# Expert layers: the two transfers of an expert's down weights issued by ScalarE on its own queue instead of by SyncE

## What is computed

```
# hier_moe: 32 experts of hidden size 512, top 2 per token; 512 tokens in layer 0, 256 in layer 1
expert_id, weights = route(h)                  # softmax over 4 groups, top 2 of the 8 experts of the best group
for each expert e with its tokens xb:          # w_gate[e], w_up[e]: 1024x512, w_down[e]: 512x1024
    y = (silu(xb @ w_gate[e]) * (xb @ w_up[e])) @ w_down[e]
out = sum over a token's two experts of weight * y
```

## Time and profile before

| | us |
|---|---|
| median of 3 runs | 3430.38 |
| lowest, highest | 3428.68, 3433.78 |
| span of the profiled execution | 3434.0 |
| PE busy in it | 2861.8 (83%) |
| PE weight loads busy | 1999.7 (58%) |
| DVE, ACT, POOL busy | 1089.5, 506.6, 253.4 |
| moved by DMA | 643.13 MB, of it 539.04 on SP's queue and 75.93 on ACT's |

### The profile page before, as it was taken

One profiled execution on the slowest core, in us unless ns is written; L12 is line 12 of the kernel. 1 busy time (PEld: TensorE's weight loads), 2 busy tenths in 40 slices (PEclk: granted clock), 3 DMA queues, 4 the chain that ended last, 5 costly groups with the idle time before them and its releaser, 6 DMA issues. The chain is left out here.

```text
span 3434.0 us, 58306 instructions
## 1 busy us (share of the span) xinstructions
PE 2861.8 (83%) x25537; PEld 1999.7 (58%) x25537; DVE 1089.5 (32%) x2184; ACT 506.6 (15%) x1104; POOL 253.4 (7%) x277
## 2 busy tenths in 40 slices
PE   6999989899898896877777379798889977877774
PEld 5887745788784444444444134388888864444442
DVE  3562363255514413100000231356556422000002
ACT  1000122100010101000000100154444310000000
POOL 0000000000000000100000110032322201000000
PEclk9999765898999997999999689799999978999997
DMA  6784120476523206899999411000000039999994
GB/s 214 236 253 133 50 92 1 136 257 185 181 74 110 62 25 239 320 390 394 396 395 400 155 62 46 18 4 4 4 3 4 4 133 380 390 398 391 395 393 167
DMA packets 284675, 643.13 MB, mean 187 GB/s; under 512 B 23540, under 2 KB 176676, under 8 KB 250772
## 3 DMA queue, kind: packets, MB, share of 16 engines
q1 hardware_dynamic: 237152, 539.04, 43.1%
q10 hardware_dynamic: 39556, 75.93, 6.1%
q0 software_dynamic: 7728, 24.59, 2.3%
HBM read 612.73 MB, written 26.77 MB: 186 GB/s over the span
## 5 line engine op out<-in xcount | busy, mean ns | idle before, releaser
L1888 PE MATMUL bank<-expert_weights,ex_xt 128*64 128x256 f32 x2688 | 352.1, 422 | 103.6 <-DMA expert_weights<-in_moe_w_up_dram 103.4
L1888 PEld LDWEIGHTS bank<-expert_weights,ex_xt 128*64 128x64 f32 x2688 | 237.6, 153 | 232.7 <-issue 160.9
L448 PE MATMUL bank<-u,weights 128*128 128x272 f32 (+1 forms) x1408 | 318.7, 390 | 14.0 <-DVEq L471 14.0
L448 PEld LDWEIGHTS bank<-u,weights 128*128 128x128 f32 x1408 | 270.8, 192 | 61.9 <-DVEq L471 14.8
L1840 DVE TENSOR_TENSOR ex_hidden<-ex_silu,bank 128x256 f32<-128x256 f32 x64 | 27.0, 422 | 685.0 <-ACT ex_silu L1924 685.0
L1888 PE MATMUL bank<-weights,ex_xt 128*64 128x256 f32 x1408 | 184.9, 423 | 58.5 <-DMA weights<-in_moe_w_up_dram 57.1
L1168 DVE SCALAR_TENSOR_TENSOR ada_acc<-ada_w,cond,ada_acc 128x512 f32 (+1 forms) x336 | 227.6, 746 | 1.5 <-PEq L420 1.5
L526 PE MATMUL bank<-rw_mixed,weights 128*128 128x512 f32 (+2 forms) x448 | 189.0, 583 | 31.7 <-DVEq L537 28.2
L1888 PEld LDWEIGHTS bank<-weights,ex_xt 128*64 128x64 f32 x1408 | 123.6, 153 | 126.5 <-issue 89.4
L1909 PE MATMUL bank<-expert_weights,ex_hidden_turned 128*64 128x512 f32 x672 | 153.5, 598 | 21.7 <-DVE ex_hidden_turned L1843 21.7
L1924 ACT ACTIVATE ex_silu<-bank 128x256 f32<-128x256 f32 x64 | 24.5, 383 | 957.7 <-PE bank L1888 957.7
(11 more groups left out here) (507 smaller groups left out, 4108.5 us busy)
## 6 DMA issues: line engine op xcount, KB each, us to landing
expert_weights<-in_moe_w_gate_dram SPq DMA_DIRECT2D x84, 1024.0 KB, 25.9
expert_weights<-in_moe_w_up_dram SPq DMA_DIRECT2D x84, 1024.0 KB, 26.6
expert_weights<-in_moe_w_down_dram SPq DMA_DIRECT2D x84, 1024.0 KB, 25.8
ada_w<-in_ada_w_dram ACTq DMA_DIRECT2D x24, 2048.0 KB, 8.8
weights<-in_moe_w_gate_dram SPq DMA_DIRECT2D x44, 1024.0 KB, 25.7
weights<-in_moe_w_up_dram SPq DMA_DIRECT2D x44, 1024.0 KB, 26.3
weights<-in_moe_w_down_dram SPq DMA_DIRECT2D x44, 1024.0 KB, 25.9
weights<-in_w_gate_dram SPq DMA_DIRECT2D x22, 1024.0 KB, 5.5
```

The source lines that it names most:

```text
L448: last = nc.tensor.matmul(k.bank[b + side * NB][:, 0:N], w[:, f, c * P:(c + 1) * P], rhs[:, f, 0:N], start=(f == 5), stop=(f == 4))
L1888: last = nc.tensor.matmul(half_cols(k.bank[2 + side], t), xt[:, s, f * SLOTS:(f + 1) * SLOTS], w[:, q * 512 + t * 256:q * 512 + t * 256 + ...
```

## The change

The loop over pieces on SP ends at piece 3 in `experts_stage`. ACT's function gets, between the copy of the tokens of e + 1 and the wait for `kept`, the issue of pieces 4 and 5 of expert e + 2, for e from 1 to 29, behind a wait for `spent` at 4(e - 1) + 4. ACT's block also moves ahead of PE's in the source, because `ring.start` enters in a table, while the program is built, the semaphore value that PE's `ring.wait` reads.

```diff
@@ block.sync
             for e in range(3, NE):
-                for j in range(ring.PIECES):
-                    sp.wait_ge(spent, 4 * (e - 3) + (1, 1, 2, 2, 3, 4)[j])
+                for j in range(4):
+                    sp.wait_ge(spent, 4 * (e - 3) + (1, 1, 2, 2)[j])
                     ring.start(sp, k.a, l, e, j)
@@ block.scalar (the whole block moved ahead of block.tensor)
                 nc.scalar.activation(act_out[:, s, :], k.bank[2][:, 0:256], ACT.Silu).then_inc(silued, 1)
                 if e + 1 < NE:
                     copy(e + 1)
+                if 3 <= e + 2 < NE:
+                    act.wait_ge(spent, 4 * (e - 1) + 4)
+                    for j in range(4, ring.PIECES):
+                        ring.start(act, k.a, l, e + 2, j)
                 act.wait_ge(kept, e + 1)
                 for n in range(2):
                     act.dma_start(out_rows[e * SLOTS:(e + 1) * SLOTS, n * 512:(n + 1) * 512],
                                   y[n * RH:(n + 1) * RH, s, :]).then_inc(put[s], 16)
```

More of the change, by code:

```diff
@@ L1863, in _, with copy @@
                                 route.ids[:, t:t + 1], None).then_inc(scattered, 16)
+        @block.scalar
+        def _(act):
+            def copy(e):
+                act.wait_ge(turned, e + 1)
+                nc.scalar.activation(xt[:, e % 2, :], k.bank[e % 2][:, :], ACT.Copy).then_inc(copied, 1)
+            copy(0)
+            for e in range(NE):
+                s = e % 2
+                act.wait_ge(spent, 4 * e + 2)
+                nc.scalar.activation(act_out[:, s, :], k.bank[2][:, 0:256], ACT.Silu).then_inc(silued, 1)
+                if e + 1 < NE:
+                    copy(e + 1)
+                if 3 <= e + 2 < NE:
+                    act.wait_ge(spent, 4 * (e - 1) + 4)
+                    for j in range(4, ring.PIECES):
+                        ring.start(act, k.a, l, e + 2, j)
+                act.wait_ge(kept, e + 1)
+                for n in range(2):
+                    act.dma_start(out_rows[e * SLOTS:(e + 1) * SLOTS, n * 512:(n + 1) * 512],
+                                  y[n * RH:(n + 1) * RH, s, :]).then_inc(put[s], 16)
+                if e == 4:
+                    act.wait_ge(scattered, 32 * route.TT)
+                    act.wait_ge(destined, route.placed)
+                    behind = route.slot_token[NE * SLOTS:, :].rearrange("(b s) o -> s (b o)", s=SLOTS)
+                    with nc.allow_non_contiguous_dma(reason="token numbers, one overflow block a column"):
+                        act.dma_start(route.slots[0:SLOTS, NE:route.nblk], behind).then_inc(listed, 16)
+                    act.dma_start(route.tab[:, :, :], route.tab_i[0:16, :]).then_inc(listed, 16)
+            for s in range(2):
+                act.wait_ge(put[s], 32 * (NE // 2))
+            act.wait_ge(listed, 32)
         @block.tensor
@@ L1912, in _ @@
                     last.then_inc(spent, 1)
[L1914 to L1940, removed]
 def overflow_stage(k, route, out_rows):
```

## The result

| us | before | after |
|---|---|---|
| median of 4 runs each | 3430.73 | 3464.36 |
| lowest, highest | 3428.68, 3433.78 | 3461.02, 3464.48 |
| span of the profiled execution | 3434.0 | 3462.7 |
| layer 0, first silu to last copy of y | 512.6 | 529.1 |
| layer 1, the same | 515.5 | 530.4 |

The kernel became slower: ratio 1.0093, 95% interval 1.0079 to 1.0107, 33.6 us more. Forecast were 3456 and 25.5 us more; the result lies within the range. Between the profiled executions the two layers differ by 16.5 and 14.9, together 31.4 us, and the rest of the span by -2.7. Of the medians' 33.6 us the profiles thus place 31.4 in the layers; 2.2 they do not place.

A forecast was written before the change was run, and what follows sets the result against it. Transfers were taken to set the pace in both layers. Layer ends 21.6, PE's clock 3.4 and layer 0's hole 0.5 sum to 25.5 us, on the median of 3430.4 to 3456 us; range 3438 to 3468.

The forecast's parts named there:

- downs-ahead case: Layer ends: down always early, an up piece lands last, tail 9.3 instead of 4.0 us; 3441 us, chance 0.17.
- SP's four remaining issues: SP's queue: SP loses two of six issues per expert but only waited for room, 0 us.
- Bandwidth in the middle: Middle of both layers: the two queues never run dry together, so total DMA time stays, 0 us.
- that rival: Middle of both layers: two queues keep the engines fuller, 418 instead of 394 GB/s; 3407 us, chance 0.08.
- The y write's lateness: ACT's queue: y writes behind down may land 20 us or more later, only DVE's copy waits, 0 us.
- ACT's issues as such: ACT, each expert: two more issues, 1.2 us, hidden, 0 us; uncovered 70 us.
- The hole at layer 0's start: Start of layer 0: down issued later leaves the queue short of work, 0.5 us, between 0 and 2.
- The step that was mis-sized: the tail: Layer ends: down lags, PE ends at E + 14.8 instead of E + 4.0 (E: before's last landing); 21.6 us for both.
- The clock's share: Layer ends: PE's clock falls in a wait of 3 to 6 us, 1.7 us per layer, 3.4 together.
- Slower still: Mixed streams lose 1%, or ACT blocks at its own full queue: 5 to 12 us more, 3461 to 3468; chance 0.05.
- some ten: Within a layer: after some ten experts, gate/up's 12 slots are full and PE waits for down instead of up.
- 17 us apart: Middle of the layers: silu starts stay 17 us apart; over 0.3 off 17.0 would disprove unchanged bandwidth.

The follow-up runs named there:

- (1): The changed kernel with the two y writes of each expert issued by SP instead of ACT: 3449.26 us, ratio 1.0051 against before.
- (2): The changed kernel with gate and up sent as 4 KB packets, two per partition, instead of 8 KB: 3456.93 us, ratio 1.0074 against before.
- (7): The changed kernel with the reads of token numbers and table issued by SP behind gate/up of expert 7, not by ACT: 3457.24 us, ratio 1.0064 against before.
- (3): The kernel before with gate and up sent as 4 KB packets, two per partition, instead of 8 KB: 3442.14 us, ratio 1.0037 against before.
- (4): The changed kernel with the down pieces of experts 28 to 31 issued by SP in its own order: 3442.64 us, ratio 1.0034 against before.

## Why the prediction was right, and by how much it was off

**The mechanism stands.** In the window 2915:3365 of after the queues moved

```profile
DMA packets 35622, 177.36 MB, mean 394 GB/s; under 512 B 4229, under 2 KB 4229, under 8 KB 22126
...
q1 hardware_dynamic: 15162, 110.40, 62.3%
q10 hardware_dynamic: 18360, 59.82, 34.6%
```

18360 to 15162 is 1.21; the count from the code was 40 to 32, 1.25. Both queues get through the same experts in the mean, so this ratio is that of the demand. That turns are equal shows in the windows further down and in what each change of packet counts did: 8 packets less for ACT (1) and 32 more for SP (2) turned the wait from down to up. The Trainium skill, DMA: Bandwidth & Descriptors, section Queues, rings and completion order, has an engine drain a whole packet, typically 9 to 17 descriptors, of one queue before it switches. Read as in the prediction, with one transfer's part on an engine as such a packet, that would have given the kernel after the tails of some 9.4 us of the downs-ahead case; it has 16.3 and 19.7, and the trace does not agree. Whether the two queues alternate packet by packet or in equal batches is not shown: the counts of a window would be the same.

**What was costed at nothing.** SP's four remaining issues: nothing. Bandwidth in the middle: 394 GB/s in both kernels, right; that rival is out. The y write's lateness: DVE waited 114.2 us for it in all (row below), and no wait of PE for `ex_y` is in the trace. ACT's issues as such: nothing where its queue has room (0.38 to 0.58 us each), but not where it is full (below). The hole at layer 0's start, 0.5 us: not seen.

```profile
DVE ex_y L1847 <- DMA slot_rows<-ex_y: 114.2, 15, 10.2
ACT ex_silu L1875 <- issue: 102.5, 4, 42.1
```

**The step that was mis-sized: the tail.** The prediction let "the second down piece of 29" land "a period after that of 28, … at least 19 us on", and had PE do two experts and a half behind it, clock included 12.5 us more than before per layer. Measured are 12.3 in layer 0 and 15.7 in layer 1: 28.0 against 25.0. The last wait was for the second piece of *28*, at 3367.98, 21.8 us before the last landing. For 29 PE did not wait: its down matmuls begin 12.9 us after that wait, behind DVE's copy alone. The queues of after in the windows 3368:3372 and 3372:3381 show why:

```profile
q1 hardware_dynamic: 158, 1.16, 69.9%
q10 hardware_dynamic: 158, 0.53, 33.1%
...
q10 hardware_dynamic: 832, 2.74, 78.8%
q1 hardware_dynamic: 112, 0.78, 20.8%
```

While both have work it is 158 packets to 158 in 4 us, the equal turns at their plainest. Then gate and up run out, ACT's queue has the engines nearly to itself, and it gets 92 packets per us (832/9) instead of 40: the next down pieces came at over twice the rate of the shared stretch. From the last wait to the last copy PE took 3.68 us for half of a down at clock 0.50 (row of the window 3368:3371.5; 1.8 at full clock) and then 38.0 us for three experts, 41.5 together, overlaps taken off. The clock's share was well set: 1.9 us there against 1.7.

That the tails came out near the forecast is in part luck. From the last wait to the last landing it reckoned 11.9 us, and the runs show 24.7 in layer 0 (1873.8 to 1898.5) and 21.8 in layer 1; from the same wait to the last copy it reckoned 28.4 (1.8 + 24.9 + 1.7), and they show 41.1 and 41.5. Both were too short by one expert, for the last wait came one expert earlier, and the two errors nearly cancel: 16.5 was forecast for the difference, 16.3 and 19.7 are measured.

**The step that was left out: ACT at a full queue.** The prediction had ACT's two issues at "hidden, 0 us", and a full queue only among "Slower still", with 0.05. In the 28 us before 1451.70 ACT had issued nine transfers (two downs of two pieces, two y writes of two, and the token numbers); the oldest of them, of 1423.88, took 30.3 us to land. The tenth issue was held 27.29 us. The oldest had landed 2.5 us into the hold, so the number of unfinished transfers alone does not say when an issue goes through; what the queue counts no run shows, and "full" is read from the long issue itself. The hold in layer 0 cost 4.2 us by the time of the landing, 5.6 by (7).

Together: 25.5 + 3.0 (tails) + 2.9 (ahead of the landings, 3.4 less the 0.5 of the hole) = 31.4, and the 2.2 that the profiles do not place make 33.6.

**The signs it named.** L1941 waits for down and L1920 for no transfer: so it was. It first waited at expert 4 (3.65 us in layer 0, 3.93 in layer 1), then steadily from expert 9 in layer 0 and 10 in layer 1, near the "some ten" of the prediction (layer 1 has one wait more, at expert 7). The first one:

```profile
1443.14 3.06 PE L1941 MATMUL bank<-expert_weights,ex_hidden_turned 128*64 128x512 f32 x8 [3.65 <-DMA expert_weights<-in_moe_w_down_dram]
```

Down's landing over 25 us, gate/up's less: 33.4, 15.0, 20.7. The tail of some 15: 16.3 and 19.7. The last two gaps of silus short: three rows of 12.46 spacing. But "17 us apart" was wrong as a test. The silu starts of after in the window 2915:3365 are

```profile
L1875 ACT ACTIVATE ex_silu<-bank x26: 383/383/384, 2916.5 to 3355.9; 128x256 f32<-128x256 f32 x26
```

the three silus of the timeline above follow at 3379.02 and later, so these are experts 3 to 28: 439.4/25 = 17.6 us apart, many of them 12.5 and most others 17 to 23.5 after the one before. By the text that would have meant less bandwidth, while the bandwidth was the same. Before, the same silus went from 2903.3 to 3329.8, 17.1 us apart. PE simply fell 0.5 us per expert behind the stream, 12.9 us in 25 experts, which is most of the tail seen from the other side.

**What stays open.** Why the landings of (1), (2) and (3) end 1.5 to 6.9 us per layer later than in before was not tried further. Nor was it settled why the median of (4) is 14 us better than its profiled execution.

## What to carry to other kernels

Before a stream of transfers is spread over two queues, count the packets of each per step of the work: here the engines took equal numbers of both while both had work, and the queue with more packets set the pace for its kind of data, whatever its bytes. In a stage that is bound by transfers the time of the last landing hardly moved with the order (here +4.2 and -0.8 us of some 510), but the order decides what is left to compute after it: look at the tail of the stage, not at the sum of the waits (188.9 us for down on one queue cost 9.7 us, 166.0 on two cost 33.6). And keep an engine that computes away from a queue that can fill up.

## What was not expected of the hardware

- An issue behind many unfinished transfers holds the issuing engine: 27.29 us in layer 0 and 12.96 in layer 1 for one transfer of ACT's, where 0.4 to 0.6 us is usual. The earlier trace rows show 2.2 to 2.3 us for two of SP's issues, but single ones of the kernel before took up to 7.98 (an up piece in layer 1). The held queue had the 4-byte token numbers ahead: in the window 1470:1492 it got 2224 packets through for 3.94 MB, SP's 404 for 2.90 MB.
- Packets of 4 KB instead of 8 KB for gate and up cost the kernel before 11 us (3442.14 against 3431.0) on one queue with nothing else changed in the order. The two layers take 517.1 and 517.3 us in its profile, 6.3 more together; where the rest lies is not shown.
- Two mixed streams with waits for up (1) landed 2 to 3 us later per layer than one stream of the same bytes, at 392 GB/s in the middle of layer 1 against 394.
